# A hybrid decoder block in float32: the factor sums of its FFNs move behind the sixth weight group, and ScalarE keeps raw pieces

## What is computed

```python
def swiglu(x, wg, wu, wd):
    return (jax.nn.silu(x @ wg) * (x @ wu)) @ wd

h = layer_norm(DN_ALPHA * h + 0.5 * swiglu(h, ffn1_wg[l], ffn1_wu[l], ffn1_wd[l]), ln1_g[l], ln1_b[l])
mix = token_mixer(h, w_in[l], ...)
h = layer_norm(DN_ALPHA * h + mix, ln2_g[l], ln2_b[l])
h = layer_norm(DN_ALPHA * h + 0.5 * swiglu(h, ffn2_wg[l], ffn2_wu[l], ffn2_wd[l]), ln3_g[l], ln3_b[l])
```

## Time and profile before

| | |
|---|---|
| median of 3 runs | 2176.2 us (2175.06 to 2176.49) |
| the profiled execution, its own time | 2173.46 us |
| its span, first to last instruction | 2171.7 us |
| TensorE (PE) busy | 2136.9 us, 98% |
| VectorE (DVE) busy | 1734.4 us, 80% |
| ScalarE (ACT) busy | 1310.4 us, 60% |
| mean granted TensorE clock | 0.995 of full |

### The profile page before, as it was taken

How to read it: one execution, slowest core, us unless ns; L and a number is a source line. 1 busy time by engine, 2 the same in 40 slices (tenths; PEclk the granted TensorE clock), 3 DMA queues, 4 the chain that set the end, 5 groups by cost and what they waited for, 6 DMA issues and landing times.

```text
span 2171.7 us, 25619 instructions
## 1 busy us (share of the span) xinstructions
PE 2136.9 (98%) x9556; PEld 1771.3 (82%) x9556; DVE 1734.4 (80%) x1438; ACT 1310.4 (60%) x1303; POOL 169.9 (8%) x281
## 2 busy tenths in 40 slices
PE   8999999999999999999999999998999999999997
PEld 6888888888887888888888888886888888888886
DVE  7799999999977567677776465658899999999986
ACT  5677777777752544454545344434677777777761
POOL 0111111111010000000000000000111111101110
PEclk9999999999999999999999999999999999999999
DMA  8688888888764555555455555555678888898862
GB/s 349 233 289 273 272 268 282 264 284 298 259 242 146 203 205 172 173 185 186 153 173 192 193 196 188 217 204 203 232 233 272 269 269 293 289 301 276 291 249 85
DMA packets 97372, 508.17 MB, mean 234 GB/s; under 512 B 13440, under 2 KB 13824, under 8 KB 56704
## 3 DMA queue, kind: packets, MB, share of 16 engines
q1 hardware_dynamic: 81216, 433.50, 54.0%
q0 software_dynamic: 16064, 73.42, 15.4%
HBM read 493.23 MB, written 13.63 MB: 233 GB/s over the span
## 4 chain that ended last, share of the span: by engine, by line
PE 95%; DVE 2%; DMA 1%; ACT 0%; issue 0%; SPq 0%; POOL 0%; DVEq 0%; ACTq 0%
PE acc L1635 11%; PE acc L1634 11%; PE acc L1633 11%; PE acc L1696 11%; PE acc L1698 11%; PE acc L1697 11%; PE tb L1698 9%; PE tb L1697 9%; PE tb L1696 9%; PE tb L1681 1%; DMA g_raw<-in_groups 1%; DVE g_lo L1030 1%; DVE act_sb L1296 0%; DMA raw<-in_stream 0%; PE tb L1957 0%; PE tb L1971 0%
## 5 line engine op out<-in xcount | busy, mean ns | idle before, releaser
L1030 DVE TENSOR_TENSOR g_lo<-g_raw,g_hi 128x2048 fp32r<-128x2048 f32 x370 | 837.9, 2284 | 120.9 <-ACT g_hi L637 120.3
L637 ACT ACTIVATE g_hi<-g_raw 128x2048 fp32r<-128x2048 f32 x370 | 706.5, 1916 | 263.1 <-PE acc L1698 82.8
L1007 DVE TENSOR_TENSOR w_lo<-raw,w_hi 128x1024 fp32r<-128x1024 f32 x272 | 326.9, 1220 | 170.7 <-ACT w_hi L597 167.3
L597 ACT ACTIVATE w_hi<-raw 128x1024 fp32r<-128x1024 f32 x272 | 279.0, 1057 | 165.0 <-PE acc L1635 99.4
L1633 PE MATMUL acc<-w_hi,xT_hi 128*128 128x512 f32 x768 | 302.2, 393 | 0.0
L1635 PE MATMUL acc<-w_hi,xT_lo 128*128 128x512 f32 x768 | 299.4, 390 | 0.0
L1634 PE MATMUL acc<-w_lo,xT_hi 128*128 128x512 f32 x768 | 299.2, 390 | 0.0
L1696 PE MATMUL acc<-g_hi,xF_hi 128*128 128x512 f32 x696 | 273.3, 393 | 15.4 <-DVE g_lo L1383 9.1
L1697 PE MATMUL acc<-g_lo,xF_hi 128*128 128x512 f32 x696 | 272.0, 391 | 0.0
L1698 PE MATMUL acc<-g_hi,xF_lo 128*128 128x512 f32 x696 | 272.0, 391 | 0.0
L1696 PE MATMUL tb<-g_hi,xF_hi 128*128 128x512 f32 x568 | 221.0, 389 | 0.0
(11 more groups left out here) (148 smaller groups left out, 2866.1 us busy)
## 6 DMA issues: line engine op xcount, KB each, us to landing
g_raw<-in_groups SPq DMA_DIRECT2D x262, 1024.0 KB, 7.0
raw<-in_stream SPq DMA_DIRECT2D x272, 512.0 KB, 4.4
g_raw<-in_groups POOLq DMA_DIRECT2D x48, 1024.0 KB, 8.0
bounce<-h_sq POOLq DMA_DIRECT2D x44, 256.0 KB, 4.9
h_in<-bounce POOLq DMA_DIRECT2D x176, 64.0 KB, 2.7
ln_gb<-in_ln SPq DMA_DIRECT2D x6, 1024.0 KB, 5.3
g_raw<-in_groups SPq DMA_DIRECT2D x4, 512.0 KB, 7.6
res<-in_x_rows SPq DMA_DIRECT2D x1, 2048.0 KB, 16.4
```

Of the source, the lines that this page charges most:

```text
L597: act.activation(w_hi[:, seg.split(j)], raw[:, seg.raw(j)], ACT.Copy).then_inc(hi_ready, 1)
L637: act.activation(g_hi[:, n % RING], source[:], ACT.Copy).then_inc(g_hi_ready, 1)
L1007: dve.tensor_tensor(w_lo[:, s], raw[:, seg.raw(j)], f32(w_hi[:, s]), ALU.subtract).then_inc(lo_ready, 1)
L1030: dve.tensor_tensor(g_lo[:, n % RING], source[:], f32(g_hi[:, n % RING]), ALU.subtract).then_inc(g_lo_ready, 1)
```

## The change

1. `factors` stands behind the low part of group 5 (the sixth), and no longer behind group 4.
2. `factors_hi` stands behind the high part of group 7.
3. Of the low parts of the factors, that of S1 is made at the end of chunk 0, those of S3, S2, S4 in chunk 1, behind P2's low part. TensorE waits for S1's before P5 and for the others before P6; its fills wait for the sums themselves.
4. In chunk 1, VectorE's weight sums are put in another order: T1, then T2 behind u1's low part and ahead of the gating, T3 and T4 behind P6's low part (they were T1, T3, T2 close together, and T4).
5. In the second FFN, `after_norm` gives ScalarE four copies `keep_raw` of the first round of transposes into raw_F, and VectorE's two rebuilding additions go. A copy waits for VectorE's low part of the same bank, and the transposes of the second round wait for the copies.

```diff
@@ -84,6 +84,7 @@
            "ub": ("u", 3)}
 FULL_SUMS = ("T1a", "T3a", "T2a", "T2b", "T4b")
 HALF_SUMS = ("T1", "T3", "T2", "T4")
+FIRST_SUMS = ("T1", "T2", "T3", "T4")
 TAIL = ((8, 3), (9, 0), (9, 1), (9, 2), (10, 0), (10, 1), (10, 2), (9, 3), (10, 3))
 
 
@@ -129,7 +130,7 @@
                 for name in rows_of(b):
                     self.row_no[f, b, name] = rows
                     rows += 1
-                for name in FULL_SUMS if is_full(b) else HALF_SUMS:
+                for name in FULL_SUMS if is_full(b) else FIRST_SUMS if b == 1 else HALF_SUMS:
                     sums += 1
                     self.sum_no[f, b, name] = sums
                 n += len(groups)
@@ -607,20 +608,31 @@
                 act.wait_ge(tr_full, filled)
                 act.activation(dst, tb[:, bank].rearrange("p (b n) -> p b n", b=BLK), ACT.Copy).then_inc(lhs_hi, 1)
 
-            def after_norm(t0, ahead, dst_hi):
+            def after_norm(t0, ahead, dst_hi, keep=None):
 
                 def piece_hi(n):
                     t, p = NORM_ORDER[n]
                     block_hi(dst_hi(p, t), 2 * t + p % 2, t0 + n + 1)
+
+                def keep_raw(n):
+                    t, p = NORM_ORDER[n]
+                    if keep:
+                        act.wait_ge(lhs_lo, b_ln2 + n + 1)
+                        act.activation(keep(p, t), tb[:, 2 * t + p % 2].rearrange("p (b n) -> p b n", b=BLK),
+                                       ACT.Copy).then_inc(s_raw, 1)
 
                 ahead(0)
                 piece_hi(0)
                 ahead(1)
                 piece_hi(1)
                 ahead(2)
+                keep_raw(0)
                 piece_hi(2)
+                keep_raw(1)
                 piece_hi(3)
+                keep_raw(2)
                 ahead(3)
+                keep_raw(3)
                 piece_hi(4)
                 piece_hi(5)
                 ahead(4)
@@ -666,8 +678,7 @@
                     k = G.load_at[f, 0, g]
                     loaded(k)
                     g_split(G.first[f, 0] + g, g_raw[slot_of[k]])
-                    if g == 6:
-                        factors_hi(f)
+                factors_hi(f)
 
             def split(f, b, name, load):
 
@@ -991,7 +1002,8 @@
                     loaded(k2 + g)
                     g_split(n2 + g, g_raw[slot_of[k2 + g]])
 
-            after_norm(t_ln2, up_ahead, lambda p, t: piece(p, t)[0])
+            after_norm(t_ln2, up_ahead, lambda p, t: piece(p, t)[0],
+                       lambda p, t: raw_F[:, (S2, S3)[t], GK * p:GK * (p + 1)])
             ffn(1)
 
 
@@ -1108,14 +1120,22 @@
             def first_block(f):
 
                 b = 1
+                qa, ra, ua = (source(f, b, name) for name in ("qa", "ra", "ua"))
                 lo_group(f, b, "P1", "qa")
-                half_sums_before(f, b)
+                load_done(f, b, "ra")
+                split_done(f, b, "P1")
+                add(qa, qa, ra)
                 lo_group(f, b, "P5", "qa")
-                second_half_sum(f, b)
                 lo_group(f, b, "P2", "ga")
+                factors_lo(f, 1, 4)
+                lo_group(f, b, "u1", "rb")
+                load_done(f, b, "ua")
+                split_done(f, b, "P5")
+                add(qa, qa, ua)
                 gate_rows(f, 0)
-                lo_group(f, b, "u1", "rb")
                 lo_group(f, b, "P6", "qa")
+                dve.wait_ge(t_ready, G.sum_no[f, b, "T1"])
+                add(ra, ra, ua)
                 fourth_half_sum(f, b)
                 lo_group(f, b, "u3", "ub")
                 lo_group(f, b, "P7", "ra")
@@ -1229,10 +1249,7 @@
                     x11, x21 = (x_stage[:, 0:2 * GK, t * P:(t + 1) * P] for t in range(TT))
                     x12, x22 = (x_stage[:, 2 * GK:4 * GK, t * P:(t + 1) * P] for t in range(TT))
                 else:
-                    dve.wait_ge(lhs_lo, b_ln2 + 8)
-                    for n, s_n in ((A11, S2), (A21, S3)):
-                        dve.tensor_tensor(raw_F[:, s_n], f32(xF_hi[:, n]), f32(xF_lo[:, n]), ALU.add).then_inc(s_raw, 1)
-                    dve.wait_ge(s_raw, 2)
+                    dve.wait_ge(s_raw, 4)
                     x11, x21 = raw_F[:, S2], raw_F[:, S3]
                     x12, x22 = (tb[:, 2 * t:2 * t + 2].rearrange("p a (b n) -> p (a b) n", b=BLK) for t in range(TT))
                 dve.tensor_tensor(raw_F[:, S1], x21, x22, ALU.subtract).then_inc(s_made, 1)
@@ -1244,9 +1261,9 @@
                 dve.tensor_tensor(raw_F[:, S4], x12, raw_F[:, S2], ALU.add).then_inc(s_made, 1)
                 dve.wait_ge(s_made, m + 4)
 
-            def factors_lo(f):
-
-                for n, s_n in enumerate((S1, S3, S2, S4)):
+            def factors_lo(f, first, last):
+
+                for n, s_n in enumerate((S1, S3, S2, S4)[first:last], first):
                     dve.wait_ge(x_hi, 7 + 4 * f + n + 1)
                     dve.tensor_tensor(xF_lo[:, s_n], raw_F[:, s_n], f32(xF_hi[:, s_n]), ALU.subtract).then_inc(x_lo, 1)
 
@@ -1254,10 +1271,9 @@
 
                 for g in range(4, 8):
                     g_lo_of(G.first[f, 0] + g, g_raw[slot_of[G.load_at[f, 0, g]]])
-                    if g == 4:
+                    if g == 5:
                         factors(f)
-                    if g == 6:
-                        factors_lo(f)
+                factors_lo(f, 0, 1)
 
             def ffn(f):
 
@@ -1774,11 +1790,13 @@
                 b = 1
                 X, Y, Z, W = (tb[:, bank] for bank in (BX, BY, BZ, BW))
                 product_group(f, b, "P1", X, A11, begin=True)
+                pe.wait_ge(x_lo, 8 + 4 * f)
                 product_group(f, b, "P5", W, S1, begin=True)
                 wait_fork(f, b, 0)
                 product_group(f, b, "P2", Y, A12)
                 wait_fork(f, b, 1)
                 plain_group(f, b, "u1", (Z, W), 1)
+                pe.wait_ge(x_lo, 11 + 4 * f)
                 product_group(f, b, "P6", X, S2)
                 plain_group(f, b, "u3", (Z, W), 3)
                 wait_fork(f, b, 2)
@@ -1880,7 +1898,7 @@
                 if f:
                     pe.wait_ge(acc_out[1], 2 * u1_end)
                 plain_half(f, 1, {}, {})
-                pe.wait_ge(x_lo, 11 + 4 * f)
+                pe.wait_ge(s_made, 4 * f + 4)
                 fill(tb[:, BY])
                 fill(tb[:, BZ])
                 first_block(f)
@@ -1895,6 +1913,8 @@
                 pe.wait_ge(ln_ready, r0 + n + 1)
                 if b0 or n >= 4:
                     pe.wait_ge(lhs_lo, b0 if n < 4 else b0 + n - 3)
+                if r0 == 10 and n >= 4:
+                    pe.wait_ge(s_raw, n - 3)
                 turn(2 * t + p % 2, [res[:, t, p * COLS + k * P:p * COLS + (k + 1) * P] for k in range(BLK)])
 
             def turns_before(seg, r0, b0):
```

## The result

The changed kernel takes **2179.01 us** (median of 22 runs) against 2175.85 us of the kernel before on the same chip (22 runs). The ratio is 1.0014, with a 95% interval of 1.0008 to 1.0020: 3.0 us slower, 1.7 to 4.4. (One of the 22 runs was disturbed, at 5619 us; without it the median is 2178.90 us, and the ratio leaves it out.) The forecast was 2179.4 us, +3.2.

A forecast was written before the change was run, and what follows sets the result against it. TensorE is busy 98% of the span, so only its waits and slow clock offer time. Two new waits with clock loss less the old hole, 2 x (3.5 + 2.1) - 8.0 = +3.2, on 2176.2 give 2179.4 us; range 2175.0 to 2182.8.

The forecast's parts named there:

- Term 1, the hole: Second FFN, chunk 0: TensorE's 6.4 us wait for group 5's low part and 1.5 us slow clock go, -8.0 us.
- The edits at no cost: ScalarE's raw copies, moved high parts and fills cost nothing; the dropped additions' 2.35 us lie inside Term 1.
- Term 2, the fork: Chunk 1, both FFNs: TensorE newly waits at u1 for ScalarE's copy of bank W to Z, +3.5 us each.
- the fork sits behind the latter's data: Chunk 1, ScalarE: the copy of bank W to Z stands behind P6's high part, which waits for T2.
- Term 3, u3: Chunk 1, both FFNs: u3's low part comes 0.7 us late each, unless TensorE has lost as much in between.
- u3 on top of the lost clock: Rival: u3's wait uncovered and larger clock loss, +5.6 us, 2181.8 us; chance 0.2.
- Term 4, the clock: Behind the new u1 waits TensorE's clock falls, costing 0 to 2.6 us each; 2.1 taken, covering u3's 0.7.
- That the clock stays up: Rival: no clock fall behind the u1 waits, only waits of 3.5 + 0.7 us each; +0.4, 2176.6 us; chance 0.1.
- That the new wait does not come: Rival: no wait at u1 in chunk 1, only the old hole goes; 2168.2 us, faster; chance 0.12.
- the forecast's own stretch: Both u1 waits come, with clock loss between 1.5 and 2.6 us: +2.0 (2178.2) to +4.2 (2180.4); chance 0.58.

The follow-up runs named there:

- third: Changed kernel with VectorE's chunk 1 reordered: two factor low parts in idle slots, one behind u3, u1 behind T2; 2169.12 us, ratio 0.9968 to the kernel before.
- ninth run: The kernel with VectorE's reordered chunk 1 (factor low parts in idle slots, u1 behind T2), unchanged, measured again; 2168.89 us, ratio 0.9969 to the kernel before.
- the fourth: Changed kernel, but all four factor low parts at the end of chunk 0 and VectorE's old chunk 1; 2171.12 us, ratio 0.9981 to the kernel before.
- sixth kernel: Changed kernel without ScalarE's raw copies, the two rebuilding additions back on VectorE; 2180.12 us, ratio 1.0023 to the kernel before.
- first experiment: Changed kernel with ScalarE's second fork (bank W to Z) moved ahead of P6's high part; 2181.33 us, ratio 1.0028 to the kernel before.
- change again: The changed kernel itself, measured once more in a later sitting; 2177.66 us, ratio 1.0010 to the kernel before.
- fifth: The change in the second FFN only, the first FFN as in the kernel before; 2173.22 us, ratio 0.9990 to the kernel before.
- second: Changed kernel with S3's factor low part moved between T1 and P5's low part; 2175.84 us, ratio 1.0001 to the kernel before.
- eighth: The kernel before with only the four raw copies on ScalarE replacing VectorE's two additions; 2174.65 us, ratio 0.9994 to the kernel before.

## Why the prediction was right

**Term 1, the hole: right.** No wait over 0.5 us is left in chunk 0. The change with its chunk 1 mended (third and ninth run) gains 7.0 and 6.7 us where 8.0 were reckoned, within both intervals, and the fourth gives -4.1 where its profile adds up to -4.2. In all profiles of kernels with the new chunk 0 the matmuls gain 8.0 us at this place. A hole of 6.4 us does give back its slow clock too.

**The edits at no cost: right, and worth more than was said.** The copies delay nothing that TensorE waits for: the transposes of the second round wait 0.70 us in the profile before and in that after. The prediction put the gain from the dropped additions inside term 1. The sixth kernel shows that they count a second time: VectorE is in arrears through chunk 1 as well, and with the additions the wait at u1 is 1.5 us longer. The change without the copies is 2.0 to 2.8 us slower than with them (+5.0 against +3.0 and +2.2 in two sittings).

**Term 2, the fork: right in place and size.** From the start of P2's low part to the start of T2 I had 62.25 - 54.42 = 7.83 us; the trace has 64.83 - 57.01 = 7.82. The wait costs 3.45 and 3.46 us, for 3.5. But the sentence "the fork sits behind the latter's data" names the first thing that is late, not the only one. The first experiment took the fork out of that queue and gained nothing (+6.1 us against +3.0), since u3's low part stands at the end of VectorE's list. The cause is the list: three low parts of factors and u1 ahead of T2, where VectorE has nothing to spare, and idle slots of 2 us left empty two steps earlier.

**Term 3, u3: right that it is covered.** After 3.45 + 1.46 us lost at u1 no wait stands at u3. Without the cover it is 3.7 us (first experiment): the 0.7 of the prediction, plus the 3.5 that TensorE is no longer late, less the 0.4 that it now waits at P6, is 3.8. The rival "u3 on top of the lost clock" didn't come.

**Term 4, the clock: right as a mean, in part by luck, and blind to its spread.** Behind the waits of 3.3 us at u1 the slow steps cost 1.46, 1.44, 1.44, 3.01, 1.50 and 2.94 us in four profiles, on average 2.0 where I took 2.1. With that mean the sum is 2 x (3.46 + 1.97) - 7.97 = +2.9 us; measured +3.0 and +2.2. The profile of the change alone would have given +1.8. The working leaned on lengths (2.03 us left the clock up, 3.16 did not), and as a rule that was wrong; the next but one section has the cases. It also took the 1.5 us behind the hole as the price of a fall. That was what was left of one: most of the low clock had gone by while TensorE still waited. That the middle between this 1.5 and the 2.6 of the norm came so near to the mean of six is luck.
By the Trainium skill (TensorE: Matmul & The Clock Gate, "Part 1: The HAM clock gate"), the number of slow matmuls at the start of one kernel changes from run to run among 6, 11 and 14. The trace agrees in that the number changes, here behind a wait: 7 slow steps behind the second wait of the changed kernel in one execution, 15 in another.

**The rivals.** That the clock stays up gave 2176.6 us: it fell in both waits of both profiles. That the new wait does not come was right only of another kernel, the third. The measured +3.0 lies in the forecast's own stretch, +2.0 to +4.2. Its interval of 1.7 to 4.4 lies wholly on the slower side of zero: the change costs a little, it is not neutral.

## What to carry to other kernels

When work is moved past a queue's other members, follow each of them to who waits, and also what stands behind the *waiting* instruction on the next engine: here a sum made 7.8 us behind a low part delayed a copy that needs nothing of it. Look for the slots in which the loaded engine idles for its partner, and fill these with the moved work before putting it in the full part of its list; and put what another engine waits for ahead of what is wanted later. The same operations, placed so, turned +3.0 us into -7.0. If taking away one wait only makes the next one as long, the bound is the engine behind both.

## What the hardware showed that was not expected

The length of an idle stretch of TensorE did not decide whether its clock fell from 2.4 to 1.2 GHz, nor what the fall cost. The low clock can begin before the wait is over, and then part of it passes while TensorE has nothing to do. The view by windows (columns as above) shows it. The first two rows are the kernel before, in the last part of the hole, which ended at 1511.55, and behind it. The third is the changed kernel's second profile, behind the wait at u1 that ended at 1543.68:

```profile
1507.80:1511.50 3.70, 0.00 (x0) 0.00 (x0) 3.63 (x4) 3.35 (x3) 0.00 (x0) 0.50 0.00 0
1511.50:1514.60 3.10, 3.05 (x7) 2.47 (x8) 3.10 (x2) 0.57 (x1) 0.00 (x0) 0.50 0.51 201
1543.70:1549.80 6.10, 6.10 (x14) 4.76 (x15) 6.10 (x4) 3.41 (x2) 4.51 (x9) 0.50 0.39 134
```

The table has the cases by idle time before the matmul: where the low clock (0.50 in the windows) begins against the end of the wait, how much of it is left behind that end, and what the slow steps lost. Not in it are the idle stretches of 3.0 to 3.5 us at the first norm, behind or in which the clock fell in all eleven profiles, and those of 3.5 to 3.6 us at the second norm with the later load, where it fell in all five.

| idle, us | where | low clock begins, us | left behind the wait, us | lost, us |
|---|---|---|---|---|
| 1.62 and 1.71 | old chunk 1 (fourth) | never | 0 | 0.09, 0.08 |
| 2.03, 2.04, 2.17 | second norm: before, first, fourth | never | 0 | 0.1 (before) |
| 2.03, 1.95, 1.95 | second norm: fifth, change, change again | 1.4, 1.3, 1.2 after | 3.4 | 1.6 |
| 2.16 and 2.17 | u1, one in idle (second) | 0.8 and 0.4 after | 3.4 | 1.71, 1.71 |
| 3.3, four times | u1, change and kin | 0.5 to 0.6 before | 2.8 to 3.0 | 1.44 to 1.50 |
| 3.3, twice | u1, change again and sixth | 0.6 and 0.8 before | 6.2 and 6.1 | 3.01, 2.94 |
| 3.55 | u3, fork ahead (first), first FFN | never | 0 | 0.12 |
| 3.53 | the same, second FFN | 0.1 after | 3.4 | 1.72 |
| 3.86 | hole, copies only (eighth) | 1.2 before | 5.6 | 2.73 |
| 4.84 | u1, old additions (sixth) | 2.6 before | 4.3 | 2.10 |
| 6.26 | hole, before | 3.7 before | 3.1 | 1.55 |

The last two columns belong together. A step takes 0.43 us at the low clock and 0.23 at the full one, so each microsecond of low clock in which TensorE works costs 0.47 us. With 0.1 for the first steps behind any wait, which are slow even where the clock stays up, this gives every loss of the table within 0.1 us: 0.47 x 3.1 + 0.1 = 1.56 for the hole, 0.47 x 6.2 + 0.1 = 3.0 for the wait at u1 that lost 3.01. That is why the longest stretch lost hardly more than most of the stretches of 3.3 us.

The case of 1.95 us in the changed kernel, where the clock was still up right behind the wait and fell later:

```profile
1480.89 0.66 PE L1697 MATMUL tb<-ident,res 128*128 128x128 f32 x4 [1.95 <-DVE res L1318]
...
1482.08 0.54 PE L1649 MATMUL acc<-w_hi,oT_hi 128*128 128x512 f32 x1
1482.42 0.63 PE L1650 MATMUL acc<-w_lo,oT_hi 128*128 128x512 f32 x1
```

What is not settled is whether a fall comes and when. The second norm has the same idle time of 2.03 us in the kernel before, without a fall, and in the fifth, with one; and 3.55 and 3.53 us at the same place of one kernel lost 0.12 and 1.72. In a sum made beforehand, each stretch of 2 to 6 us in this stream of matmuls is therefore to be priced with 0 to 3 us for the clock. That spread is also a reason why one profile of this kernel can stand a us or more beside its median.
